# Two layers of attention: the softmax's product by the reciprocal on ScalarE, and one pair of key heads copied by VectorE

## The reference

```python
def mla_branch(...):                     # 8 heads, 64 + 32 wide keys, 64 wide values, causal
    k_nope = (ckv @ w_uk).reshape(B, S, MLA_HEADS, MLA_NOPE)
    v = (ckv @ w_uv).reshape(B, S, MLA_HEADS, MLA_V)
    ...
    s = (qn @ k_nope + qr @ k_rope) * scale          # per head, causal mask
    p = jax.nn.softmax(s, axis=-1)
    return p @ v
def memory_branch(...):                  # 4 heads, 128 wide, no mask, keys from `mem`
    p = jax.nn.softmax(q @ k * MEM_HDIM ** -0.5, axis=-1)
    return p @ v
def hgrn2_branch(...):                   # gated recurrence, 4 heads
    ...
x = x + (gates[0] * y_mla + gates[1] * y_hg + gates[2] * y_mem) @ w_out
```

## Time and profile before

| | us |
|---|---|
| median of 3 runs | 2363.22 (2362.87 to 2363.33) |
| the profiled execution | 2360.51 |
| its span in the trace | 2358.7 |
| PE busy | 2339.2 (99%) |
| DVE busy | 1644.9 (70%) |
| ACT busy | 1243.7 (53%) |
| POOL busy | 361.6 (15%) |

### The profile page before, as it was taken

The page is one execution under the profiler, slowest core; times in us unless marked ns, Lnnn a source line. Parts: engine busy times, 40 slices in busy tenths (PEclk is TensorE's granted clock), DMA queues, the critical chain, the costliest instruction groups (busy, mean ns, idle before and its releaser), DMA issues.

```text
span 2358.7 us, 51046 instructions
## 1 busy us (share of the span) xinstructions
PE 2339.2 (99%) x21836; PEld 2280.1 (97%) x21836; DVE 1644.9 (70%) x2292; ACT 1243.7 (53%) x1788; POOL 361.6 (15%) x313
## 2 busy tenths in 40 slices
PE   9999999999999999999999999999999999999998
PEld 9999999999999999999999999989999999989998
DVE  7775787866667657878766766776765766776764
ACT  6554656654445456565454544635554544635553
POOL 4012020300200210203003002431002002431001
PEclk9999999999999999999999999999999999999999
DMA  7555533555555545335555645422555555422653
GB/s 255 195 197 190 178 119 141 179 197 196 194 184 196 197 179 179 122 131 180 211 182 196 223 179 197 167 81 91 215 179 197 197 179 197 172 76 92 214 182 123
DMA packets 57681, 410.22 MB, mean 174 GB/s; under 512 B 6384, under 2 KB 6640, under 8 KB 8688
## 3 DMA queue, kind: packets, MB, share of 16 engines
q1 hardware_dynamic: 56592, 402.15, 47.9%
q10 hardware_dynamic: 864, 4.82, 0.5%
HBM read 405.89 MB, written 1.05 MB: 173 GB/s over the span
## 4 chain that ended last, share of the span: by engine, by line
PE 87%; DVE 5%; issue 3%; ACT 3%; POOL 1%; DMA 0%; SPq 0%; DVEq 0%; POOLq 0%; ACTq 0%
PE bank L325 86%; DVE sb_wlo L338 2%; DVE area L338 2%; ACT area L334 2%; PE bank L329 1%; POOL sb_x_ssq L338 1%; ACT sb_whi L334 0%; DVE area L366 0%; DMA sb_raw<-stream 0%; POOL area L338 0%; POOL sb_x_sq L338 0%; DVE area L376 0%; DVE area L349 0%; SPq L419 0%; ACT L334 0%
## 5 line engine op out<-in xcount | busy, mean ns | idle before, releaser
L325 PE MATMUL bank<-area,sb_whi 128*128 128x256 f32 x11752 | 2018.7, 278 | 3.3 <-ACT sb_whi L334 1.8
L325 PEld LDWEIGHTS bank<-area,sb_whi 128*128 128x128 f32 x11752 | 1770.0, 188 | 13.4 <-DVE area L338 2.9
L325 PE MATMUL bank<-area,sb_wlo 128*128 128x256 f32 x5876 | 1607.4, 277 | 3.9 <-DVE sb_wlo L338 3.6
L334 ACT ACTIVATE sb_whi<-sb_raw 128x1024 fp32r<-128x1024 f32 x762 | 794.0, 1056 | 620.8 <-PE bank L325 608.5
L325 PEld LDWEIGHTS bank<-area,sb_wlo 128*128 128x128 f32 x5876 | 1095.9, 188 | 6.5 <-DVE sb_wlo L338 6.5
L338 DVE TENSOR_TENSOR sb_wlo<-sb_raw,sb_whi 128x1024 fp32r<-128x1024 f32 x762 | 956.8, 1266 | 161.4 <-ACT sb_whi L334 159.8
L338 DVE TENSOR_TENSOR area<-area,area 128x256 f32<-128x256 f32 (+6 forms) x504 | 257.8, 523 | 193.3 <-ACT area L334 191.0
L334 ACT ACTIVATE area<-area 128x256 fp32r<-128x256 f32 (+5 forms) x487 | 230.6, 482 | 90.4 <-DVE area L338 79.1
L338 DVE TENSOR_TENSOR area<-bank,sb_x_diag 128x512 f32<-128x512 f32 x244 | 167.1, 685 | 68.6 <-PE bank L325 56.8
L325 PE MATMUL bank<-area,area 64*64 64x64 f32 (+5 forms) x2864 | 151.0, 250 | 0.2
L334 ACT ACTIVATE area<-bank 128x512 f32<-128x512 f32 (+5 forms) x154 | 76.0, 505 | 141.4 <-PE bank L329 81.0
(11 more groups left out here) (82 smaller groups left out, 720.1 us busy)
## 6 DMA issues: line engine op xcount, KB each, us to landing
sb_raw<-stream SPq DMA_DIRECT2D x379, 1024.0 KB, 4.8
sb_raw<-stream SPq DMA_DIRECT2D x4, 512.0 KB, 7.5
area<-lora ACTq DMA_DIRECT2D x2, 768.0 KB, 6.5
area<-c ACTq DMA_DIRECT2D x1, 1504.0 KB, 7.8
sb_x<-x SPq DMA_DIRECT2D x4, 256.0 KB, 5.9
area<-mem ACTq DMA_DIRECT2D x1, 1024.0 KB, 6.7
out<-sb_x SPq DMA_DIRECT2D x4, 256.0 KB, 2.9
area<-m ACTq DMA_DIRECT2D x1, 512.0 KB, 3.7
```

The costliest lines, as they stand in the source:

```text
L325: return lambda e: e.matmul(out, lhsT, rhs, start=start, stop=stop, skip_group_check=True, tile_position=at)
L334: return lambda e: e.activation(out, a, f, **kw)
```

## The change

In `normalise` the two multiplications by the reciprocal are ACT copies with a scale read from SBUF; the reciprocal stays on DVE, and ACT waits for it. `turn` waits for ACT alone. In `heads_project` the second unit of key heads (`kn`, `i = 1`) is evacuated by two DVE copies, and the first scores wait for them.

```diff
     def heads(dst, i, name):
         def evacuate(u, b, count):
             src = b[:, :].rearrange("p (n t) -> p n t", n=2)
+            if name == "kn" and i:
+                dve.wait(pe, count)
+                dve.run(tensor_copy(dst[0:64, 4 * i:4 * i + 4:2, :], src[0:64]))
+                n = dve.mark(tensor_copy(dst[0:64, 4 * i + 1:4 * i + 4:2, :], src[64:128]))
+                k.emptied[u] = (dve, n)
+                m.done["kn", 1] = n
+                return
             act.wait(pe, count)
             act.run(activation(dst[0:64, 4 * i:4 * i + 4:2, :], src[0:64], ACT.Copy))
             m.done[name] = act.mark(activation(dst[0:64, 4 * i + 1:4 * i + 4:2, :], src[64:128], ACT.Copy))
@@
     def scores(s):
         if s == 0:
             pe.wait(act, max(m.done["qn"], m.done["kn"], m.k_rot_done))
-            pe.wait(dve, m.done["qr"])
+            pe.wait(dve, max(m.done["qr"], m.done["kn", 1]))
@@
         n = dve.mark(reciprocal(m.rc[:, c], m.sm[:, c]))
-        dve.wait(dve, n)
+        act.wait(dve, n)
         for q, (a, z) in enumerate(parts if s < 8 else ((0, T), (T, 2 * T))):
             i = 2 * s + q
-            ready[s] = dve.mark(tensor_scalar(p[:, a:z], p[:, a:z], m.rc[:, i:i + 1], ALU.mult))
+            ready[s] = act.mark(activation(p[:, a:z], p[:, a:z], ACT.Copy, scale=m.rc[:, i:i + 1]))
@@
         p, pt = m.p[s % 2], m.pt[s % 2]
-        pe.wait(dve, ready[s])
-        if s >= 1:
-            pe.wait(act, copied[s - 1])
+        pe.wait(act, ready[s])
```

## The result

| | before | after |
|---|---|---|
| median, us | 2362.46 (6 runs, 2360.15 to 2363.33) | 2376.65 (6 runs, 2374.99 to 2377.45) |
| ratio | | 1.0063, 95% interval 1.0053 to 1.0074 |
| profiled execution / span, us | 2360.51 / 2358.7 | 2377.11 / 2375.3 |

The account below looks back on a forecast made before the run. A chain over DVE and ACT was taken to hold PE from step 5. Delays of 1.85 us by step 1 and 6.24 in steps 2 to 7 give 8.1 a layer, 16.2 in all: 2379.4 us (+0.69%), 8-in-10 range 2373 to 2384.

Parts of the forecast that it names:

- the term for step 1: Step 1 of `attend`: 0.94 us carried in, plus 1.04 on ACT, less 0.13 before DVE was free: 1.85 us delay.
- The chain: Loop of `attend`: a chain over DVE and ACT; DVE's multiplications lie beside ACT's `late` and `early`, so moving them gains 0.
- The size of a step: Steps of `attend`: ACT's wait for the reciprocal and two copies (0.71 us) delay `late` by 1.04 us, bounds 0.88 to 1.22.
- step 8: Memory head in `attend`: 1.14 us added to DVE's first low split, taken by 1.1 us in hand; delay stays 8.1.
- The second rival: DVE's multiplications beside POOL in `attend` come apart, winning 1.28 us in each of six steps: 2364 us, chance 5%.
- Where the delay ends: Steps 9 to 11 of `attend` and behind: nothing added, nothing given back; 8.1 us a layer stay.
- PE's waits: PE in `attend` waits for low parts or DVE's multiplications about 1 us a step from step 3, some 9 a layer.
- The key heads: `heads_project`: DVE's two copies of the second pair, 1.4 us, fit a 2.03 us gap; 0 us, bounds -0.1 to +0.1.
- `turn`: PE's transposing of probabilities: they are ready 0.2 us later, with over 1 us in hand; 0 us.
- the first rival: DVE relief in `attend`: steps shorten by up to 0.47 us, PE's low-part waits go, at most 1.2 a layer; 2360.9, chance 3%.

Follow-up runs that it names:

- the wait alone: Kernel before with ACT's wait for the reciprocal added and nothing moved, multiplications still on DVE: 2364.82 us, ratio 1.0014.
- the idle copies alone: Kernel before plus two idle ACT copies, shaped and placed like the moved multiplications, from a constant to their own buffer, without a wait: 2372.39 us, ratio 1.0040.
- the kernel before with POOL's wait: Kernel before with POOL's addition of a level made to wait for DVE's two multiplications of that level: 2356.04 us, ratio 0.9978.
- the key heads alone: Kernel before with only the second pair of key heads moved to DVE, multiplications not moved: 2360.78 us, ratio 1.0000.

## Why the forecast was right, and its term that was off

**The number.** 2379.4 us was forecast, 2376.65 measured. Of the 2.7 us between them 0.8 is the median of the kernel before, which came to 2362.46 over six runs, and 2.0 the loss itself, 14.2 us and not 16.2. The mechanism held; what was off is the term for step 1.

**The chain.** That DVE and ACT bound the loop together, with ACT's `late` and `early` the later arm, is shown: the same copies cost 14 us ahead of the two and nothing behind them.

**The size of a step.** 1.04 us a step was forecast from the exponentials' rows and 0.03 us hand-overs; 0.99 to 1.05 us came in steps 2 to 7 (6.12 in sum, where 6.24 was forecast), and in step 8 the 1.14 that was forecast. The copies took 0.81 us, and 0.71 to the next start, as the exponentials' rows said. The rule of the Trainium skill (ScalarE: Activation LUTs, "Rules for kernel authors") to multiply on VectorE comes out right in its sign where the copies stand ahead of the chain; its ground, the rate per element, priced a step at 0.16 us. The runs show 1.04 us with the copies ahead of the chain and none behind it.

**Step 1, mis-sized.** 1.85 us of delay at the end of step 1 was forecast; it measured 318.56 - 315.26 - 2.07 = 1.23 us at the next maximum. The step of the forecast was "1.04 us on ACT; but level 0 has only `late`". DVE's multiplication of level 0 in the kernel before, with POOL beside it:

```profile
309.63 2.49 POOL L338 TENSOR_TENSOR area<-area 128x512 f32<-128x512 f32 x2 [41.52 <-ACT area L334]
309.68 1.54 DVE L338 TENSOR_TENSOR area<-area,area 128x512 f32<-128x512 f32 x1
```

and in the changed kernel:

```profile
313.70 0.69 DVE L338 TENSOR_TENSOR area<-area,area 128x512 f32<-128x512 f32 x1 [1.42 <-ACT area L334]
313.75 2.67 POOL L338 TENSOR_TENSOR area<-area 128x512 f32<-128x512 f32 x2 [43.57 <-ACT area L334]
```

Before, DVE was held by its own multiplications of `m.p` and came 0.05 us behind POOL; its one operation took 1.54 us. In the changed kernel it stood waiting, came 0.05 us ahead, and took 0.69. That is 0.85 us a layer given back. The rest of step 1 adds up around it: the multiplication starts 313.70 - 309.68 - 2.07 = 1.95 us late and not 1.85, and POOL, now later, lies beside the low splits, which take 2.46 us and not 2.35; 1.95 - 0.85 + 0.11 is 1.21 of the 1.23. With the 6.12 of steps 2 to 7 that makes 7.35, and at the low part at 370.34 PE is 379.75 - 370.34 - 2.07 = 7.34 us late, where 8.1 was forecast. The second rival's mechanism was real, and I had ruled it out with "both start from ACT's `late` and `early`, and keep their distance". In level 0 DVE's start didn't come from ACT. The kernels with the wait alone and with the idle copies alone show the same: DVE's multiplication of level 0 takes 0.69 us in both, and the first of them has step 1 shorter for it. In the kernel before, POOL's first operation ends at 310.67 and DVE's, which started second, at 311.22. The rule of the Trainium skill (SBUF — State Buffer, its table row on running DVE and GpSimd together) that the second to issue waits for the first agrees with these four rows, and with the pair's 2.53 and 1.29 us.

**Where the delay ends.** Nothing was to be added in steps 9 to 11 or given back behind. DVE's step 9 did grow, by 0.94 us, but little of it reached PE, and step 10 is 1.53 us shorter than before (8.71 against 10.24), where DVE had waited for PE. PE is 7.34 us late at step 8 and 9.62 - 2.07 = 7.55 at 391 us, measured at the same matmuls; 8.0 us at 424 us in the first layer, and 7.1 us over the stretch in the second. Sum 15.1 us, less what lies between the stretches, 14.5 us at the end. The few tenths gained and lost there were not traced.

**PE's waits.** "Some 9 us a layer" were to be seen; 9.4 are, all in `attend`. That is in the rows of the weight loads. In those of the matmuls, from which the forecast had its 1.2 us of before, it is 7.0 (4.9 and 2.1). The lengths of steps 2 to 7 were put at "some 10.1 us"; they are 10.0 to 11.0, since the added 1.04 holds for each step and not the sum.

**The other parts.** The key heads cost nothing, as costed. The probabilities were in time for `turn`: no wait of PE on ACT of more than 0.33 us appears in the changed kernel's `attend`.

**What was wrong beside the forecast:** the price of the first rival. It was given 1.2 us a layer for PE's waits; the kernel before with POOL's wait shows 2.5 to 2.7 when they go, not all of it explained. That changed neither sum nor range.

## What to carry to other kernels

An engine with idle gaps isn't relieved by taking work from it that lies in a gap: look at what ends the wait *behind* the work, and if it is the engine that is to take the work over, its place in that queue decides, not its busy share. If a short product must go to the other engine, queue it behind what the chain waits for, if its own reader can wait that long. Where two engines' SBUF work costs double when side by side, a start that shifts by a tenth of a microsecond can be worth nearly one; read the pair's duration with and without the neighbour before calling the distance fixed.

## What the runs showed that was not expected

- The order in which DVE and POOL start: 0.05 us either way make 0.85 us, and one wait on POOL made the kernel before 0.22% faster (0.13 to 0.30% by the interval), though POOL is busy for 15% of the span and no engine's wait in `attend` is put down to it.
- Executions differ by up to 4 us before the first attention stretch: against the trace of the kernel before, the same matmul near 281 us comes 0.6 us earlier (the wait alone) to 3.5 us later (the key heads alone). In these windows of the first 30 us the granted clock, as a share of 2.4 GHz, is the last column but two. The kernel before, then the changed one:

```profile
10.00:20.00 10.00, 10.00 (x65) 9.89 (x65) 6.32 (x11) 5.97 (x11) 4.57 (x4) 0.72 0.76 295
20.00:30.00 10.00, 9.84 (x87) 9.44 (x86) 6.07 (x8) 7.07 (x10) 3.38 (x5) 1.00 0.94 351
```

```profile
10.00:20.00 10.00, 9.69 (x78) 9.12 (x77) 5.95 (x10) 5.41 (x10) 4.90 (x4) 1.00 0.81 314
20.00:30.00 10.00, 7.75 (x53) 7.23 (x53) 4.05 (x6) 5.09 (x8) 3.02 (x5) 0.83 0.91 328
```

  The stretch at the lower clock (1.2 GHz, 0.50 in windows of 2 us) lies in the first window of the one and in the second of the other, where PE is also idle for 2.25 us of the 10, most of it ahead of the slow stretch (busy for 0.88 and 1.25 us of the windows of 2 us from 22 and 24 us). The 2.07 us come about between 22 and 30 us; that the place of the slow stretch is their cause is not shown. The kernel with the key heads alone has it like the changed kernel (0.83 in the second window), and reaches the same matmuls 2.0 us later than before at 30 us and 3.5 us later at 281 us, but loses nothing more in the 2080 us behind. So a span difference of 2 us between two single executions of this kernel says nothing; a difference of step lengths does.
